# Two projection chunks at first, block by block, in a streaming encoder layer on one Trainium2 core

## What is computed

```
m = silu(c) @ w_ada + b_ada -> shift1, scale1, gate1, shift2, scale2, gate2
h = LN0(x) * (1 + scale1) + shift1
[u | q | k | v] = h @ w_in          (each part 512 wide, so w_in is 1024 x 2048)
a = trailing means of u (windows 2, 4, 8, 16 on 4 groups of 128 channels) minus u,
    a 128 x 128 map for each group, a scale for each channel
s = stick-breaking attention over (q, k, v)
x = LN1(alpha * x + gate1 * ([a | s] @ w_o)), then a SwiGLU part and LN2
```

## Time and profile before

| | |
|---|---|
| runs (us) | 2556.46, 2560.21, 2561.23; median 2560.21 |
| the profiled execution | 2559.0, its span 2557.3 |
| busy: PE, DVE, ACT, POOL | 94%, 57%, 41%, 35% |
| mean granted TensorE clock | 0.98 of full |
| first stage and projection | 0 to about 483 us of the span |
| attention and the rest | from there to the end |

### The profile page before, as it was taken

The page is one execution under the profiler, slowest core; times in us unless marked ns, Lnnn a source line. Parts: engine busy times, 40 slices in busy tenths (PEclk is TensorE's granted clock), DMA queues, the critical chain, the costliest instruction groups (busy, mean ns, idle before and its releaser), DMA issues.

```text
span 2557.3 us, 36195 instructions
## 1 busy us (share of the span) xinstructions
PE 2401.7 (94%) x14148; PEld 1326.5 (52%) x14148; DVE 1450.3 (57%) x1934; ACT 1047.0 (41%) x1629; POOL 888.0 (35%) x1030
## 2 busy tenths in 40 slices
PE   4899899899999889999999999999999999999998
PEld 3445455444444444455555554446666544688733
DVE  4747655488888887768777774405333203433214
ACT  2522233499999995234555553102222200133200
POOL 2300000277777773324666767301111340111100
PEclk7899999899999999999999999999999999999999
DMA  7214868433323112231556547754454445466555
GB/s 252 85 50 169 283 234 268 139 100 83 100 83 83 34 67 86 83 111 73 164 201 201 207 165 268 260 176 147 147 166 133 136 136 189 154 220 201 189 165 167
DMA packets 214308, 394.58 MB, mean 154 GB/s; under 512 B 30157, under 2 KB 150285, under 8 KB 205562
## 3 DMA queue, kind: packets, MB, share of 16 engines
q1 hardware_dynamic: 197146, 330.40, 39.3%
q10 hardware_dynamic: 16992, 61.87, 7.7%
HBM read 301.92 MB, written 90.30 MB: 153 GB/s over the span
## 4 chain that ended last, share of the span: by engine, by line
PE 52%; POOL 9%; DVE 6%; ACT 5%; issue 4%; DMA 4%; DVEq 0%; POOLq 0%; SPq 0%; ACTq 0%
PE ps L2612 20%; PE ps L2651 15%; PE ps L2477 6%; DMA dn_dram<-work 3%; POOL work L973 3%; DVE work L1792 2%; PE ps L2352 2%; PE ps L2368 2%; PE ps L2329 2%; POOL work L901 2%; ACT work L1209 2%; ACT ps L1221 1%; PE ps L2562 1%; POOL work L948 1%; POOL work L946 1%
## 5 line engine op out<-in xcount | busy, mean ns | idle before, releaser
L2612 PE MATMUL ps<-hidden_t,work 128*128 128x384 f16 (+1 forms) x4608 | 669.4, 307 | 17.9 <-ACT work L1363 17.1
L2612 PEld LDWEIGHTS ps<-hidden_t,work 128*128 128x128 f16 x4608 | 449.3, 98 | 234.9 <-DVE work L1969 21.1
L2651 PE MATMUL ps<-work 128*128 128x512 f16 x2244 | 473.2, 380 | 6.4 <-DVE work L2062 3.7
L2236 PE MATMUL ps<-hidden_t,work 128*128 128x416 f16 x1920 | 352.1, 344 | 12.8 <-DVE hidden_t L1557 8.2
L901 POOL TENSOR_TENSOR work<-work 128x512 f32<-128x512 f32 (+2 forms) x320 | 307.6, 964 | 134.8 <-DVE work L1792 78.1
L2651 PEld LDWEIGHTS ps<-work 128*128 128x128 f16 x2244 | 206.4, 98 | 271.9 <-issue 28.7
L973 POOL TENSOR_TENSOR work<-work 128x384 f16<-128x384 f32 (+1 forms) x116 | 121.0, 1047 | 501.2 <-ACT work L1388 501.2
L2236 PEld LDWEIGHTS ps<-hidden_t,work 128*128 128x128 f16 x1920 | 189.6, 99 | 162.8 <-issue 16.5
L1792 DVE TENSOR_TENSOR_SCAN work<-ps,work 128x512 f32<-128x512 f32 x192 | 237.3, 1270 | 26.8 <-ACT ps L1221 25.8
L862 POOL TENSOR_TENSOR work<-work,col 128x1 f32<-128x1 f32 x68 | 33.2, 488 | 534.4 <-DVE work L1542 534.4
L2329 PE MATMUL ps<-work 128*128 128x512 f16 (+3 forms) x640 | 174.5, 356 | 37.8 <-DVE work L1792 29.8
(11 more groups left out here) (262 smaller groups left out, 2865.1 us busy)
## 6 DMA issues: line engine op xcount, KB each, us to landing
work<-dn_dram ACTq DMA_DIRECT2D x96, 512.0 KB, 3.6
work<-gs_dram SPq DMA_DIRECT2D x88, 512.0 KB, 4.1
work<-gs_dram SPq DMA_DIRECT2D x44, 768.0 KB, 4.3
work<-in_w_ada SPq DMA_DIRECT2D x24, 1024.0 KB, 5.3
work<-in_w_gu SPq DMA_DIRECT2D x22, 1024.0 KB, 5.9
work<-in_w_gu SPq DMA_DIRECT2D x44, 512.0 KB, 5.1
gs_dram<-work SPq DMA_DIRECT2D x22, 1024.0 KB, 6.8
gs_dram<-work SPq DMA_DIRECT2D x66, 256.0 KB, 4.9
```

What stands on the lines that cost most here:

```text
L2236: mm = pe.matmul(ps[:, blk, 0:PB], B_HL[s][:, wh * KD * P + k * P:wh * KD * P + (k + 1) * P], hidden_t[:, k, xh, PB * blk:PB * (blk + 1)], ...
L2612: mm = pe.matmul(ps[:, bank, 0:n], w, x, start=(q in (1, 2, 5) and k == 0 and (wh, xh) == (0, 0)), stop=(k == 3 and (wh, xh) == TERMS[-1]) ...
L2651: mm = pe.matmul(ps[r:r + rows, 2 * slot + half, :], E_HID[:, j, xh, at:at + rows], E_DHL[slab_home(g)][:, wh, 512 * half:512 * (half + 1) ...
```

## The change

- TensorE projects chunks 0 and 1 together, block by block, in blocks of 512, 512, 512, 272 and 272 tokens (`RAMP`) that match the token groups: (chunk 0, block 0), (chunk 1, block 0), (chunk 0, block 1) and so on, in banks 0 to 3 in turn. The transposes of later groups stand between the blocks.
- Chunk 2 has weight halves of its own (`B_HL[2]`), and chunks 0, 1 and 3 u buffers of their own; chunk 2 uses chunk 0's. The loads of w_in chunks 2 and 3 are issued ahead of the sample tile's.
- VectorE and ScalarE split chunk 0 within the first group, chunk 1 right behind it, and chunk 2 within the last.
- `mod_turn`: the 16 small products that turn the modulation rows are spread behind the w_ada products, into bank 0; the first four transposes go ahead of the last two w_ada products.
- `mix_pool` and `wpool_evac` are cut into pieces that stand between the blocks of chunks 2 (for g = 0), 3 (1), 4 and 5 (2) and 6 (3). `store_pool(3)` is issued in chunk 6.
- `pool_rows` 0 follows `prep_low(2)`; `pool_rows` 1, 2 and 3 follow the preparation of chunks 4, 5 and 6.
- Two of the weight maxima go with chunks 4 and 5 each in place of four, four with chunks 8 to 11 in place of three; the total is the same.

The core of the diff:

```diff
+        RAMP = [(0, 512), (512, 512), (1024, 512), (1536, 272), (1808, 272)]
...
-        MAX_OF = [0] * 4 + [4] * 4 + [3] * 7 + [1]
+        MAX_OF = [0] * 4 + [2] * 2 + [4] * 6 + [3] * 3 + [1]
...
             for t in range(NT + 1):
                 rstd_a(t)
+                if t == 5:
+                    weight_max(1)
+            weight_max(2)
...
             for c in range(4, 8):
                 u = c % 2
-                next_w(c, u)
+                next_w(c)
+                if c < 6:
+                    store_pool(c - 3)
                 load_maxima(c)
+                if c == 6:
+                    store_pool(3)
                 sp.wait_ge(proj_out, 5 * c + 5)
...
             group_a(0)
-            w_split(0, 0)
+            w_split(1)
             for g in range(1, 4):
                 group_a(g)
+                evac_pool(0, g - 1)
+                evac_pool(1, g - 1)
             sample_a()
+            w_split(2)
+            for blk in (3, 4):
+                evac_pool(0, blk)
+                evac_pool(1, blk)
             act.wait_ge(misc_in, 48)
-            for g in range(4):
-                w_split(g + 1, (g + 1) % 2)
-                if g:
-                    act.wait_ge(pooled_set, g)
-                    act.wait_ge(npool_mm, g + 1)
-                evac_pool(g, g % 2)
-                if g:
-                    wpool_evac(g - 1)
+            for blk in range(5):
+                if blk == 0:
+                    act.wait_ge(pooled_set, 1)
+                    act.wait_ge(npool_mm, 2)
+                evac_pool(2, blk)
...
             for c in range(4, 8):
                 u = c % 2
-                w_split(c + 1, 1 - u)
+                w_split(c + 1)
                 if c >= 6:
                     act.wait_ge(q_stored[u], 32)
                 for blk in range(5):
                     evac(c, u, B_QT[u], blk)
+                    if c == 4 and blk >= 3:
+                        wpool_evac(2, 2 * blk - 6, 2 * blk - 4)
+                    if c == 5 and blk == 0:
+                        wpool_evac(2, 4, 5)
+                    if c == 6 and 1 <= blk < 4:
+                        wpool_evac(3, 2 * blk - 2, min(2 * blk, 5))
                 high_part(c, B_QT[u])
-            wpool_evac(3)
...
+            prep_low(2)
+            pool_rows(0)
+            last_rows(0)
+            prep_max(3)
+            prep_scale(3)
+            prep_low(3)
+            last_rows(1)
-            for c in range(16):
+            for c in range(3, 16):
                 if c < 15:
                     prep_max(c + 1)
                     prep_scale(c + 1)
                 if c < 8:
                     prep_low(c + 1)
-                if 1 <= c <= 3:
-                    pool_max(c - 1)
-                if c < 4:
-                    pool_rows(c)
-                    last_rows(c)
+                if c < 6:
+                    pool_max(c - 3)
+                    pool_rows(c - 2)
+                if c < 5:
+                    last_rows(c - 1)
...
+            def project_two(blk):
+                for c in range(2):
+                    if 0 < blk < 3:
+                        for k in range(4 * c, 4 * c + 4):
+                            turn_a(blk + 1, k)
+                    if blk == 0:
+                        weights_in(c)
+                    if blk >= 2:
+                        pe.wait_ge(proj_out, proj_n(c, blk - 2))
+                    if c == 0:
+                        pe.wait_ge(a_lo, 4 * blk + 4 if blk < 4 else 17)
+                    project_block(c, blk)
+                    if blk == 0:
+                        for k in range(6 * c, 6 + 2 * c):
+                            turn_a(1, k)
...
+                    if c == 2 and 1 <= blk < 4:
+                        mix_pool(0, 2 * blk - 2, min(2 * blk, 5))
+                    if c == 6 and 1 <= blk < 4:
+                        mix_pool(3, 2 * blk - 2, min(2 * blk, 5))
+                    if c == 3 and blk >= 2:
+                        mix_pool(1, 2 * blk - 4, min(2 * blk - 2, 5))
+                    if c == 4 and blk >= 3:
+                        mix_pool(2, 2 * blk - 6, 2 * blk - 4)
+                    if c == 5 and blk == 0:
+                        mix_pool(2, 4, 5)
```

More of the change, by code:

```diff
@@ L1088, in group_a @@
                         high_a(g, q - 1)
+                if g == 0:
+                    w_split(0)
                 high_a(g, 3)
@@ L1121, in evac, with wpool_evac @@
                                scale=c1(C_W + 2 * s + 1)).then_inc(proj_out, 1)
-            def wpool_evac(g):
-                for blk in range(5):
+            def wpool_evac(g, first, last):
+                for blk in range(first, last):
                     m = 5 * g + blk
@@ L1183, in _ @@
                 if c < 15:
-                    w_split(c + 1, 1 - s)
+                    w_split(c + 1)
                 evac(c, s, B_VT[s], 1)
@@ L1728, in _ @@
             v.tensor_copy(HIST_T, ps[:, 7, 0:4 * HIST]).then_inc(npool_out, 1)
-            own.done(v.memset(B_U[:, 0:16], 0.0))
-            step(v.memset(B_U[:, 2064:2065], 0.0))
+            for g in (0, 1, 3):
+                own.done(v.memset(B_U[g][:, 0:16], 0.0))
+                own.done(v.memset(B_U[g][:, 2064:2065], 0.0))
+            own.wait()
             v.wait_ge(npool_out, 1)
-            for c in range(16):
+            prep_low(2)
[5 more added lines that the diff above has]
+            last_rows(1)
+            for c in range(3, 16):
                 if c < 15:
@@ L2193, in turn_a, with mod_turn @@
                 mm.then_inc(a_tr, 1)
+            def mod_turn(s):
+                pe.wait_ge(ada_row, s + 1)
+                for q in (2 * s, 2 * s + 1):
+                    mm = pe.matmul(ps[:, 0, 2 * q:2 * q + 2], A_MROW[:, q * P:(q + 1) * P], SEL, start=True, stop=True)
+                return mm
             pe.wait_ge(ct_set, 1)
             for s in range(8):
+                if s == 6:
+                    for k in range(4):
+                        turn_a(0, k)
                 pe.wait_ge(wada_in[s // 2], 32)
@@ L2227, in project, with weights_in, project_block @@
+            def weights_in(c):
                 pe.wait_ge(w_hi, c + 1)
                 pe.wait_ge(w_lo, c + 1)
+            def project_block(c, blk):
+                at, n, bank = proj_block(c, blk)
+                for k in range(KD):
+                    for wh, xh in TERMS:
+                        mm = pe.matmul(ps[:, bank, 0:n], w_home(c)[:, wh * KD * P + k * P:wh * KD * P + (k + 1) * P],
+                                       hidden_t[:, k, xh, at:at + n],
+                                       start=(k == 0 and (wh, xh) == (0, 0)),
+                                       stop=(k == KD - 1 and (wh, xh) == TERMS[-1]))
+                mm.then_inc(proj_mm, 1)
@@ L2240, in project @@
-                    mm.then_inc(proj_mm, 1)
-                    if first and blk < 2:
-                        for k in range(KD):
-                            turn_a(blk + 2, k)
-                    if first and blk == 2:
-                        turn_sample()
+                    project_block(c, blk)
+                    if c == 2 and blk < 2:
+                        last_rows(blk)
+                    if c in (3, 4) and blk == 1:
+                        last_rows(c - 1)
+                    if c == 2 and 1 <= blk < 4:
+                        mix_pool(0, 2 * blk - 2, min(2 * blk, 5))
@@ L2251, in project, with mix_pool @@
                             token_rows(m + blk - 2)
-            def mix_pool(g):
+            def mix_pool(g, first, last):
                 pe.wait_ge(pooled_set, g + 1)
-                for blk in range(5):
+                for blk in range(first, last):
                     m = 5 * g + blk
```

212 lines of the change are left out of this document (122 added, 90 removed).

## The result

| | before | after |
|---|---|---|
| median of 14 runs each (us) | 2560.16 | 2566.22 |
| lowest, highest | 2556.46, 2562.27 | 2559.57, 2568.51 |
| ratio to before, 95% interval | | 1.0022 [1.0015, 1.0029] |
| profiled execution, its span | 2559.0, 2557.3 | 2559.57, 2557.8 |
| end of projection (marker, below) | 485.23 | 491.69 |

The changed kernel is **slower by 0.22%, some 6 us**, where 6.8 us faster had been forecast. The measurement lies outside the range.

What follows compares the result with a forecast made beforehand. TensorE (94% busy) bounds; only its idle time before 483 us can be won. 7.7 us won at the start, then 176.4 against 175.5 to chunk 8's fourth block: 6.8 us faster, 2552.2 profiled, 2553.4 predicted; range 2545 to 2562.

Steps and rivals of the forecast that it cites:

- The two chunks: Paired chunks 0 and 1 on TensorE: through at 126.8 us against 134.5, 7.7 us won.
- two round trips to GpSimd: VectorE ahead of token group 1: waits on GpSimd taken at 2.4 us in all, reaching 68.0.
- first block: Start of projection on TensorE: the first block starts at 57.0 us in place of 72.1.
- The waits: TensorE waits: 4.1 us ahead of mix_pool(1), 2.3 ahead of mix_pool(2), 5.9 inside mix_pool(3), 5.5 in chunk 8.
- almost one for one: Through chunk 8: old TensorE waits of 11.8 us return almost one for one as new waits of 17.8 us.
- Maxima with chunks 8 to 11: VectorE, four maxima in place of three: costed at nothing; without cover up to 2.2 us per chunk, 9 in all.
- The modulation chain: Start: transposing steps from 32.5 us take 3, and the chain arrives at 39.9, 2.8 us sooner.
- The blocks of 272 tokens: End of the paired chunks on TensorE: four blocks of 2.8 us each.
- The clock behind a gap: TensorE: 1.3 us charged for each gap of 4.4, 4.1 and 5.9 us, none for 2.3.
- The slower rival: TensorE's clock stays low through short bursts between 57 and 98 us: 10 us slower, 2570; chance 0.10.
- The late store: Store ahead of pool_rows(3) lands late, moving chunk 6's wait by 4.7 us: 2.1 won, 2558; chance, with its like, 0.18.
- the long second step of 1.42 us on GpSimd: Ahead of group 1: GpSimd's second step taken at 1.42 us beside prep_low(1); 0.55 would be 0.9 us sooner.

Runs made afterwards that it cites:

- e1: Changed kernel, but chunk 1's maximum over the partitions taken with chunk 0's by TensorE and VectorE, without GpSimd: 2558.76 us, ratio to before 0.9988.
- e2: Kernel before, with one unused partition maximum added on GpSimd between the rstd steps of tiles 5 and 6: 2572.60 us, ratio to before 1.0042.
- e9: Changed kernel with a second partition maximum on GpSimd directly ahead of chunk 1's: 2568.39 us, ratio to before 1.0027.
- e4: Changed kernel with pool_max(3) in chunk 7 instead of 8 and w_split(9) behind three copies of chunk 8: 2567.68 us, ratio to before 1.0021.
- e11: Changed kernel with the edits of e1 and e4, w_split(7) later, VectorE's order changed in chunks 3 and 4, four maxima in chunk 8: 2541.35 us, ratio 0.9921.
- e10: Changed kernel with chunk 1's maximum on GpSimd two places later, behind the rstd steps of tiles 6 and 7: 2565.15 us, ratio to before 1.0016.
- e5: Changed kernel with e1's edit and w_split(7) behind the first two results of mix_pool(3): 2551.22 us, ratio to before 0.9958.

## Why the prediction was wrong

**The step that failed** is in "The two chunks": ahead of group 1 "two round trips to GpSimd" were taken at "2.4 us of waits, and reach 68.0". In after these waits took 2.08 + 6.57 + 0.72 = 9.4 us, and the last normalised tile ended at 75.77 (66.66 in e1, where the forecast would have been 1.3 us too late). The term was mis-sized because it priced GpSimd's operations and not the passing from rstd to maximum and back. The change in GpSimd's order was looked at for what it makes wait, and not for what it makes change. e1, e2 and e9 show this cause: without the passing the loss goes, with it alone the loss comes, and a second maximum adds no second gap.

The earlier trace rows show rstd steps alone, and in before no maximum stands among them: the first came at 105.12, behind 10.21 us of waiting, where a gap could not show. Yet the way back could have been read from before's trace further on, where attention begins. GpSimd's timeline of before, 440 to 492 us:

```profile
440.15 0.35 POOL L867 PARTITION_ALL_REDUCE small<-small  x1 [22.60 <-DVE small L1535]
440.37 0.17 POOL L887 MEMSET col<- 128x1 f32 x1
483.63 0.29 POOL L897 TENSOR_SCALAR_AFFINE_SELECT work<-work 128x128 f32<-128x128 f32 x1 [43.10 <-ACT work L1209]
491.51 0.40 POOL L901 TENSOR_TENSOR work<-work 128x127 f32<-128x127 f32 x1 [7.59 <-DVE work L1789]
```

The first multiplication behind the last maximum is put down to VectorE, whose scan (L1789) had ended at 484.77: 6.7 us passed behind that. The same gap, of 6.78 to 7.60 us, stands there in every kernel here, behind the marker.

The milestones, TensorE's time of resuming in us:

| | predicted | after | e1 |
|---|---|---|---|
| first block | 57.0 | 58.08 | 58.79 |
| both chunks through | 126.8 | 138.5 | 127.8 |
| mix_pool(1) | 169.3 | 180.78 | 170.16 |
| mix_pool(2) | 202.3 | 214.06 | 203.28 |
| mix_pool(3) | 252.1 | 263.76 | 252.98 |
| chunk 8 | 303.2 | 315.13 | 306.90 |

Of the 11.9 us by which after resumes late in chunk 8, 11.7 are there when both chunks are through. The 7.8 us by which the last normalised tile was late are most of these; the rest is below. Everything between was forecast to a few tenths, in part because a shorter wait and a dearer clock made up for one another. In e1 the last row is 3.7 late, since chunk 8's wait was 6.84 us there, not 5.5, and the clock cost more behind `mix_pool(3)` (last section).

**Right.** The waits: 4.1, 2.3, 5.9 and 5.5 predicted; 4.17, 2.21, 4.47 and 5.69 measured, each at the place and ended by the engine named, the third 1.4 us shorter. The old waits do come back as new ones, and with more: 16.5 us for 11.8 (17.8 in the forecast's own sum, which isn't "almost one for one" either). Maxima with chunks 8 to 11 cost nothing as long as chunk 8's wait hides them; e4 and e11 show the price once that cover is gone, waits of 4.57 and 5.80 us in chunk 9 where the text had put up to 2.2 for each chunk.

**Sizes that were off.** The modulation chain ended at 41.27 in place of 39.9: the four transposing steps in it began at 33.64, not 32.5, and took 3.65 us, not 3. The blocks of 272 tokens took 12.8 us together, not 11.2, at a granted clock of 0.87. The clock behind a gap cost more than the 1.3 charged: 1.84 behind `mix_pool(1)`'s wait (3.38 for 1.88, and 4.72 for 4.38), 1.84 too behind the 2.21 us that were charged nothing (2.54 for 1.88, and 5.56 for 4.38), and 3.05 behind the 5.69 in chunk 8, where before lost some 1.7. These and chunk 8's longer wait are why e1 wins 3.3 us by its marker and not 6.8.

**Rivals.** The slower rival had the right sign by another mechanism: TensorE's clock did not stay down. Block (1, 0) took 5.34 us at 79.95, right behind the gap of 10.61 us and the transposes, and the transposes ahead of it lost 1.36 us (4.28 for e1's 2.92). Behind the gap of 4.03 us the loss was larger, 2.9 (3.68 us for 16 transposes, 6.45 for the block). The Trainium skill, "TensorE: Matmul & The Clock Gate", section "HAM oscillation", tells of short bursts that each begin cold: the trace agrees, with 1.4 to 3 us behind each of these gaps, far from the 17 of that rival. The late store did not occur: VectorE waited 1.02 us for it. Nor did the long second step of 1.42 us on GpSimd: VectorE stood idle during that of tile 6 (0.59 us), and its low part had ended when that of tile 7 began (0.55); beside the low part the first step of tile 7 took 1.12.

## What to carry to other kernels

Read an engine's list for changes of kind as well as for durations: an operation of 0.38 us, put among others of GpSimd, cost 12 us of its time (5.69 + 6.68) and decided the sign of the result. What a removed wait is worth depends on what is late next; the same edit gave 3.2 us alone and 7.0 us with others, so try removals in pairs. And work costed at nothing because a wait hides it must be costed again as soon as that wait is taken away.

## What the hardware showed that was not expected

GpSimd passes from `tensor_tensor` (with a power) to a maximum over the partitions in 5.57 to 5.75 us and back in 6.68 to 7.31 us, in after, e2, e9 and e10. In e10 the way back is put down to VectorE, whose statistics had been ready 2.2 us before it ended. Where GpSimd had been idle for about that long anyway, as at 122.75 in after, the maximum followed its input by 0.84 us. In e1, e5, e9 and e10 that maximum too starts 5.62 to 6.06 us behind the last rstd step and 0.5 to 1.0 behind its input, so the time seems to run from the end of the last operation and not from the input. Not every pair of operations has this price: a memset and an affine_select follow a maximum at once (123.16 and 124.09 in after, 440.37 in before), and affine_select and `tensor_tensor` alternate at once in attention.

The same gap costs the clock differently from one execution to the next. Behind the wait of 2.21 us ahead of `mix_pool(2)` after lost 1.84 us and e9 0.10. Behind a wait of 4.47 us inside `mix_pool(3)` the four products took 3.34 us in after and 3.75 in e1 (1.88 without a gap), and the next block 4.38 and 5.42. The granted clock of after's chunk 8, just behind its wait (the number behind POOL's):

```profile
314.00:318.00 4.00, 2.87 (x10) 1.75 (x11) 4.00 (x3) 2.17 (x4) 0.00 (x0) 0.54 0.15 46
```

That is near the lower of the two levels, as in the earlier trace rows. What sets it within these limits was not tried. Also left open: what GpSimd does in the gaps, and which other operations change with a price.
